# Second mixer: the product of probabilities and values from float32 to high and low parts in three passes

## The chip, the cores and the metric

One core of a Trainium2 chip runs the whole program once. The metric is the device time of that core in microseconds. Its five engines run programs of their own and meet at semaphores: TensorE (PE in the rows, with its weight loads as PEld), VectorE (DVE), ScalarE (ACT), GpSimd (POOL) and SyncE (SP), which issues the weight loads from memory.

## The reference, cut to what matters

Sequence 512, width 1024, float32 throughout. Two layers of feed-forward, mixer, feed-forward, and then a hybrid layer. The change lies in the mixer of the second layer, differential attention with 8 heads of width 128, where two softmaxes over 64-wide halves of queries and keys are subtracted and the difference multiplies the values:

```python
p1 = jax.nn.softmax(jnp.einsum('bhqd,bhkd->bhqk', q1b, k1) + bias, axis=-1)
p2 = jax.nn.softmax(jnp.einsum('bhqd,bhkd->bhqk', q2b, k2) + bias, axis=-1)
return jnp.einsum('bhqk,bhkv->bhqv', p1 - lam * p2, vh)
...
out = rms_norm(out, subln_g) * (1.0 - lam_init)
return out.reshape(B, S, DIFF_V).astype(h.dtype) @ w_out
```

## The kernel before

Activations lie transposed in SBUF, 128 features by 512 positions to a tile. A projection is made of units of 128 output columns. For a unit ScalarE copies 128x1024 raw weights into a float32r tile (`whi`, the high part), VectorE subtracts it from the raw weights (`wlo`, the low part), and TensorE does 24 matmuls of 512 columns in float32r: high by high, high by low, low by high. This scheme of parts is used for all projections and for the scores of the second mixer. The product of probabilities and values is not made so: its operands are plain float32.

The order of the second mixer is one list, `diff_steps()` (L231), which the programs of TensorE (L2322), ScalarE (L1062) and VectorE (L1704) each walk from front to back, doing their share of each step. Each engine is strictly in this order; a wait holds up all that stands behind it on its engine. A block n is 128 queries of head n // 4. The steps named below:

- `half`: 12 of the 24 matmuls of a projection unit (k, q or v of a head). After the second half VectorE makes the low part of a later weight unit (`w_lo`, L1334) and empties the bank (L1725 into `qb`, L1720 into `vt` for v). For k and q ScalarE squares the result.
- `ss`, `rs`, `qk`, `hi`, `lo`: TensorE sums the squares of q and k; ScalarE takes Ln and Exp of each sum (`rq`); VectorE scales (L1734); ScalarE copies six high parts (`hi`), VectorE subtracts four low parts (`lo`, L1746). `attend` of a new head needs these low parts.
- `attend` n: TensorE makes two score tiles of two matmuls each, VectorE adds the bias and takes the minimum (L1758), ScalarE exponentiates (L772).
- `comb` n: four VectorE instructions (L1787 to L1793) subtract the two softmaxes.
- `turn` n: TensorE turns the block in four transposes into one PSUM bank, and ScalarE empties the bank into its part of `DPT` (`sb_dif_pt`) and counts `d_pt`. The next `turn` needs the bank to be empty.
- `vT` h: TensorE turns the values (`dvt`), ScalarE empties the bank into `DV` and counts `d_vrow`.
- `pv` h: four float32 matmuls of `DV` and `DPT`; ScalarE squares the result. `oss` and `o` normalise it, `y` splits it for the output projection, whose rows are the steps `begin` and `more`.

From head 1 to head 5 the steps repeat, here with n = 4h:

```python
half("k", h + 1, 0)
steps += [("vT", h), ("attend", n), ("comb", n - 1), ("o", h - 2)]
half("k", h + 1, 1)
steps.append(("turn", n - 2))
half("q", h + 1, 0)
steps += [("attend", n + 1), ("comb", n), ("turn", n - 1)]
half("q", h + 1, 1)
steps += [("attend", n + 2), ("comb", n + 1), ("pv", h - 1), ("ss", h + 1)]
half("v", h + 1, 0)
steps += [("rs", h + 1), ("qk", h + 1), ("hi", h + 1), ("turn", n), ("attend", n + 3), ("comb", n + 2)]
half("v", h + 1, 1)
steps += [("lo", h + 1), ("oss", h - 1), ("turn", n + 1)]
```

GpSimd takes no part in this, save the loads of the bias. In the feed-forward parts it issues 75 accumulating DMAs within SBUF (L2600).

Of the kernel before, what the change touches and what calls it, by code (L numbers as in the profile page):

```python
# [51 lines left out]
NCOLS = _n  # L52
STAGE = 21792

# [347 lines left out]
d_hi_q d_hi_k d_lo_q d_lo_k d_v d_vT d_vrow  # L402
d_score d_max d_exp d_comb d_turn d_pt d_pv d_osq d_oss d_y d_yhi d_ylo
gs h_z h_hi h_conv0 h_conv h_gmm h_gates h_ri h_ix h_tanh h_a h_ln h_m h_sqrt h_one h_b h_scan
# [5 lines left out]
def build(nc, a):  # L410
    with ExitStack() as ctx:
# [74 lines left out]
        with ExitStack() as mem:  # L486
            def t_(name, shape, dt=F32):
                return sb("dif_" + name, shape, dt, mem)

            O = t_("y", [128, 8, S])  # L490
            bt = [t_(f"bias{i}", [128, 896]) for i in range(2)]
            qb = [t_(f"qb{i}", [128, S]) for i in range(2)]
            dsq = [t_(f"sq{i}", [128, S]) for i in range(2)]
            drq = [t_(f"rq{i}", [128, S]) for i in range(2)]
            dparts = [[t_(f"{n}{i}", [128, S], F32R) for n in ("q0", "q1", "k0", "k1", "kl0", "kl1")] for i in range(2)]
            dvt = t_("vt", [128, S])
            DV = [t_(f"v{i}", [128, 4, 128]) for i in range(2)]
            dpb = [[t_(f"p{i}{j}", [128, S]) for j in range(2)] for i in range(3)]
            DPT = t_("pt", [128, 4, S])
            dst = [t_(f"st{i}", [128, 8]) for i in range(3)]  # L500
# [255 lines left out]
        def act_program(e):  # L756
# [305 lines left out]
            def diff():  # L1062
                u = first["diff"]
                for s in DS:
# [41 lines left out]
                    elif s[0] == "vT":  # L1106
                        h = s[1]
                        w.wait_ge(sem["d_vT"], h + 1)
                        if h >= 2:
                            w.wait_ge(sem["d_pv"], h - 1)  # L1110
                        act(DV[h % 2][:, :, :], psum[DIF_MISC][:, :].rearrange("p (s c) -> p s c", c=128),
                            ACT.Copy).then_inc(sem["d_vrow"], 1)
                    elif s[0] == "attend":
# [6 lines left out]
                    elif s[0] == "turn":  # L1120
                        n = s[1]
                        w.wait_ge(sem["d_turn"], n + 1)
                        if n >= 4:
                            w.wait_ge(sem["d_pv"], n // 4)
                        act(DPT[:, :, n % 4 * 128:n % 4 * 128 + 128],
                            psum[DIF_TURN][:, :].rearrange("p (c q) -> p c q", q=128),
                            ACT.Copy).then_inc(sem["d_pt"], 1)
                    elif s[0] == "pv":
                        h = s[1]
                        w.wait_ge(sem["d_pv"], h + 1)  # L1130
                        if h:
                            w.wait_ge(sem["d_oss"], h)
                        act(sq[:, :], psum[DIF_PV][:, :], ACT.Square).then_inc(sem["d_osq"], 1)
                    elif s[0] == "oss":
                        h = s[1]
                        w.wait_ge(sem["d_oss"], h + 1)
                        if h:
                            w.wait_ge(sem["d_y"], h)
                        rsqrt_into(sqs[:, :], psum[DIF_MISC][:, :], 128, ("d_o", h))
# [173 lines left out]
        def dve_program(e):  # L1313
# [390 lines left out]
            def diff():  # L1704
                u = first["diff"]
                zero_halves(dparts)
                for s in DS:
                    if s[0] == "half":
                        _, tag, h, half = s
# [59 lines left out]
                    elif s[0] == "y":  # L1769
                        n = s[1]  # L1770
                        w.wait_ge(sem["d_yhi"], n + 1)
                        e.tensor_tensor(xl[:, n, :], O[:, n, :], xh[:, n, :].bitcast(F32),
                                        ALU.subtract).then_inc(sem["d_ylo"], 1)
                    elif s[0] == "begin" and s[1]:
                        w_lo(u)

            def zero_halves(parts):
# [200 lines left out]
        def pe_program(e):  # L1978
# [332 lines left out]
            def diff_misc_free(key):  # L2311
# [5 lines left out]
                elif key[0] == "vT":  # L2317
                    w.wait_ge(sem["d_vrow"], key[1] + 1)
                else:
                    w.wait_ge(sem["lnb"], ln_done(("q", key[1])))  # L2320

            def diff():  # L2322
                u = first["diff"]
                misc, in_free, got = None, [], {}
                for s in DS:
# [48 lines left out]
                    elif s[0] == "turn":  # L2374
                        n = s[1]
                        w.wait_ge(sem["d_comb"], 4 * n + 4)
                        if n:
                            w.wait_ge(sem["d_pt"], n)
                        turned(DIF_TURN, dpb[n % 3][0], 4, sem["d_turn"])
                    elif s[0] == "pv":  # L2380
                        h = s[1]
                        w.wait_ge(sem["d_vrow"], h + 1)
                        w.wait_ge(sem["d_pt"], 4 * h + 4)
                        if h:
                            w.wait_ge(sem["d_y"], h)
                        for c in range(4):
                            ins = mm(psum[DIF_PV][:, :], DV[h % 2][:, c, :], DPT[:, c, :], c == 0, c == 3)
                        ins.then_inc(sem["d_pv"], 1)
# [21 lines left out]
            def out_bank_free(m):  # L2410
# [7 lines left out]
                elif m == 5:  # L2418
                    w.wait_ge(sem["d_pt"], 32)
                elif m == 6:  # L2420
# [345 lines left out]
```

## Time and profile before

| | us |
|---|---|
| median of 3 runs (2163.63 to 2164.08) | 2163.75 |
| the profiled execution | 2163.63 |
| its span in the profile | 2161.8 |
| busy PE / PEld / DVE / ACT / POOL | 2144.5 / 1835.3 / 1680.9 / 1176.7 / 253.0 |
| share of the chain that ended last: PE, DVE, ACT | 91%, 4%, 2% |

Times in the rows are microseconds from the start of the span, those marked mean are ns. [...] A float32 matmul stands as two records. The second mixer lies between about 1310 and 1556 us, and its products stand at 1365.77, then every 27.94 us.

### The profile page before, as it was taken

The numbers are of one execution on the slowest core, as the hardware profiler recorded it, in microseconds if no ns is written. First come the engines' busy times: TensorE is split into PE (matmuls) and PEld (weight loads), VectorE is DVE, ScalarE is ACT, GpSimd is POOL, SyncE is SP. The second block draws the span as 40 slices with busy tenths as digits, with TensorE's granted clock in tenths as the row PEclk, the third lists the DMA queues.
The fourth block names the chain that finished last, engine by engine and source line by source line (L and its number), as shares of the span: only waits on it lengthen the run. The fifth ranks groups of instructions, "written<-read, shape, count | busy, mean of one in ns | idle before, by whom it ended". The sixth has DMA issues, their size and how long they took to land.

```text
span 2161.8 us, 33546 instructions
## 1 busy us (share of the span) xinstructions
PE 2144.5 (99%) x13412; PEld 1835.3 (85%) x13412; DVE 1680.9 (78%) x2546; ACT 1176.7 (54%) x1922; POOL 253.0 (12%) x187
## 2 busy tenths in 40 slices
PE   9999999999999999999999999999999999999999
PEld 6989897777779898989899997777789898977777
DVE  8789697988678796888787787777688886966873
ACT  6536264667556263546355356777555362638672
POOL 3000004000040000040010112000130000030000
PEclk9999999999999999999999999999999999999999
DMA  7454535131135555354554542222135545332211
GB/s 214 123 136 99 151 94 161 40 98 60 46 89 141 124 137 151 84 162 125 176 129 127 122 126 92 77 75 95 50 79 150 137 100 150 98 131 74 79 59 39
DMA packets 249451, 237.75 MB, mean 110 GB/s; under 512 B 4984, under 2 KB 245240, under 8 KB 249296
## 3 DMA queue, kind: packets, MB, share of 16 engines
q1 hardware_dynamic: 208336, 210.25, 30.3%
q0 software_dynamic: 40752, 25.11, 8.7%
q8 instruction: 107, 1.75, 0.3%
q14 instruction: 48, 0.39, 0.1%
q10 hardware_dynamic: 208, 0.24, 0.0%
HBM read 213.79 MB, written 6.32 MB: 102 GB/s over the span
## 4 chain that ended last, share of the span: by engine, by line
PE 91%; DVE 4%; ACT 2%; issue 1%; DMA 0%; SPq 0%; ACTq 0%; DVEq 0%
PE ps L1982 90%; PE ps L1986 1%; DVE sb_wlo L1334 1%; DMA sb_raw<-ffn_w_gu 0%; ACT sb_whi L771 0%; DVE sb_gla_ek L1689 0%; DVE sb_gla_eq L1692 0%; ACT sb_hyb_th L771 0%; ACT sb_lnb L771 0%; DVE sb_gla_cf L1681 0%; DVE sb_gla_xb L1684 0%; DVE sb_gla_d L1669 0%; SPq L737 0%; DVE sb_rb L1965 0%; ACT sb_xh L771 0%
## 5 line engine op out<-in xcount | busy, mean ns | idle before, releaser
L1982 PE MATMUL ps<-sb_xh,sb_whi 128*128 128x512 f32 (+1 forms) x1812 | 625.4, 345 | 3.6 <-issue 1.8
L1982 PE MATMUL ps<-sb_xl,sb_whi 128*128 128x512 f32 (+1 forms) x1812 | 608.8, 337 | 0.1
L1982 PE MATMUL ps<-sb_xh,sb_wlo 128*128 128x512 f32 (+1 forms) x1812 | 606.7, 337 | 0.0
L771 ACT ACTIVATE sb_whi<-sb_raw 128x1024 fp32r<-128x1024 f32 (+1 forms) x368 | 379.9, 1037 | 376.6 <-PE ps L1982 359.8
L1982 PEld LDWEIGHTS ps<-sb_xh,sb_whi 128*128 128x128 f32 x1812 | 344.0, 190 | 56.8 <-issue 20.4
L1982 PEld LDWEIGHTS ps<-sb_xl,sb_whi 128*128 128x128 f32 x1812 | 344.2, 190 | 39.3 <-DVE sb_xl L1354 3.3
L1982 PEld LDWEIGHTS ps<-sb_xh,sb_wlo 128*128 128x128 f32 x1812 | 343.9, 190 | 37.1
L1982 PE MATMUL ps<-sb_ffn_tl,sb_whi 128*128 128x256 f32 x1200 | 339.6, 283 | 0.0
L1982 PE MATMUL ps<-sb_ffn_th,sb_whi 128*128 128x256 f32 x1200 | 339.6, 283 | 0.0
L1982 PE MATMUL ps<-sb_ffn_th,sb_wlo 128*128 128x256 f32 x1200 | 339.6, 283 | 0.0
L1334 DVE TENSOR_TENSOR sb_wlo<-sb_raw,sb_whi 128x1024 fp32r<-128x1024 f32 (+1 forms) x218 | 275.6, 1271 | 49.1 <-ACT sb_whi L771 48.6
L1982 PE MATMUL ps<-sb_ffn_ah,sb_whi 128*128 128x512 f32 x704 | 275.4, 391 | 0.0
L1982 PE MATMUL ps<-sb_ffn_ah,sb_wlo 128*128 128x512 f32 x704 | 274.1, 389 | 0.0
L1982 PE MATMUL ps<-sb_ffn_al,sb_whi 128*128 128x512 f32 x704 | 274.1, 389 | 0.0
L1982 PEld LDWEIGHTS ps<-sb_ffn_tl,sb_whi 128*128 128x128 f32 x1200 | 230.4, 192 | 0.0
L1982 PEld LDWEIGHTS ps<-sb_ffn_th,sb_wlo 128*128 128x128 f32 x1200 | 230.4, 192 | 0.0
L1982 PEld LDWEIGHTS ps<-sb_ffn_th,sb_whi 128*128 128x128 f32 x1200 | 230.4, 192 | 0.0
L2600 POOL DMA_DIRECT2D sb_raw<-sb_raw x75 | 96.4, 1350 | 989.5 <-DMA sb_raw<-ffn_w_gu 736.2
L1327 DVE TENSOR_TENSOR sb_wlo<-sb_raw,sb_whi 128x1024 fp32r<-128x1024 f32 x150 | 182.7, 1218 | 2.4 <-ACT sb_whi L771 2.4
L771 ACT ACTIVATE sb_whi<-sb_ffn_sums 128x1024 fp32r<-128x1024 f32 (+1 forms) x150 | 125.7, 841 | 83.4 <-DVE sb_ffn_sums L1349 64.5
L1982 PEld LDWEIGHTS ps<-sb_ffn_ah,sb_wlo 128*128 128x128 f32 x704 | 132.1, 188 | 27.9
L1982 PEld LDWEIGHTS ps<-sb_ffn_ah,sb_whi 128*128 128x128 f32 x704 | 132.2, 188 | 26.9
(293 smaller groups left out, 2919.9 us busy)
## 6 DMA issues: line engine op xcount, KB each, us to landing
sb_raw<-ffn_w_gu SPq DMA_DIRECT2D x86, 1024.0 KB, 5.8
sb_raw<-ffn_w_down SPq DMA_DIRECT2D x32, 1024.0 KB, 5.1
sb_raw<-sb_raw POOLq DMA_DIRECT2D x75, 256.0 KB, 4.2
sb_raw<-w_ada SPq DMA_DIRECT2D x12, 1024.0 KB, 7.6
sb_raw<-ffn_w_down SPq DMA_DIRECT2D x16, 768.0 KB, 5.6
sb_raw<-gla_w_in SPq DMA_DIRECT2D x12, 1024.0 KB, 5.5
sb_raw<-diff_w_in SPq DMA_DIRECT2D x12, 1024.0 KB, 5.1
sb_raw<-w_in SPq DMA_DIRECT2D x10, 1024.0 KB, 5.1
```

What stands on the lines that cost most here:

```text
L771: return e.activation(out, in_, func, bias=bias, scale=scale)
L1327: e.tensor_tensor(lo, fast_source(u), hi.bitcast(F32), ALU.subtract).then_inc(sem["w_lo"], 1)
L1334: e.tensor_tensor(lo, raw[panel % NRAW][:, 0:nk, off:off + 128], hi.bitcast(F32), ALU.subtract).then_inc(sem["w_lo"], 1)
L1982: return e.matmul(out, lhsT, rhs, start=start, stop=stop, skip_group_check=skip)
L1986: ins = e.transpose(psum[bank][:, c * 128:(c + 1) * 128], src[:, c * 128:(c + 1) * 128], ident)
L2600: e.dma_start(raw[up % NRAW][:, 0:4, off:off + 128], raw[gate % NRAW][:, 0:4, off:off + 128], accum_op=ALU.add).then_inc(sem[f"s_pre{i % 2 ...
```

## The change

The values and the turned probabilities are kept as float32r high parts and float32r low parts, and the product becomes three float32r matmuls for each of the four blocks of keys. ScalarE empties each turned bank twice: into the high part (`DPT`, `DV`) and, exact, into a second tile (`dpw`, one buffer; for the values `dvt`, their own source). The next `turn` waits for both. VectorE subtracts the high part from the exact copy, 32 times for the probabilities (`low_probabilities`) and 8 times for the values (`low_values`), after the first `attend` or `comb` that follows the `turn` or `vT` in the list; the second copy into `dpw` waits for the subtraction of the block before. `pv` waits for the low parts. The count `d_pt` and `d_vrow` go by twos. The space for stages grows, and the memory kept for GpSimd's DMA descriptors is set to 2048 bytes a partition.

```diff
-STAGE = 21792
+STAGE = 25376
...
-            DV = [t_(f"v{i}", [128, 4, 128]) for i in range(2)]
+            DV, DVL = ([t_(f"{n}{i}", [128, 4, 128], F32R) for i in range(2)] for n in ("v", "vl"))
-            DPT = t_("pt", [128, 4, S])
+            DPT, DPTL = t_("pt", [128, 4, S], F32R), t_("ptl", [128, 4, S], F32R)
+            dpw = t_("pw", [128, 4, 128])
...
# ScalarE, vT and turn
+                        turned = psum[DIF_MISC][:, :].rearrange("p (s c) -> p s c", c=128)
+                        act(DV[h % 2][:, :, :], turned, ACT.Copy).then_inc(sem["d_vrow"], 1)
+                        act(dvt[:, :].rearrange("p (s c) -> p s c", c=128), turned, ACT.Copy).then_inc(sem["d_vrow"], 1)
...
+                        act(DPT[:, :, own], turned, ACT.Copy).then_inc(sem["d_pt"], 1)
+                        if n:
+                            w.wait_ge(sem["d_ptl"], n)
+                        act(dpw[:, :, :], turned, ACT.Copy).then_inc(sem["d_pt"], 1)
...
# VectorE
+                    if s[0] == "turn":
+                        if block is not None:
+                            low_probabilities(block)
+                        block = s[1]
+                    elif s[0] == "vT":
+                        head = s[1]
...
+                        if n == 6:
+                            low_probabilities(block)
+                            block = None
...
+                    if s[0] in ("attend", "comb"):
+                        if head is not None:
+                            low_values(head)
+                            head = None
+                        if block is not None:
+                            low_probabilities(block)
+                            block = None
+            def low_probabilities(n):
+                own = slice(n % 4 * 128, n % 4 * 128 + 128)
+                w.wait_ge(sem["d_pt"], 2 * n + 2)
+                e.tensor_tensor(DPTL[:, :, own], dpw[:, :, :], DPT[:, :, own].bitcast(F32),
+                                ALU.subtract).then_inc(sem["d_ptl"], 1)
+            def low_values(h):
+                w.wait_ge(sem["d_vrow"], 2 * h + 2)
+                e.tensor_tensor(DVL[h % 2][:, :, :], dvt[:, :].rearrange("p (s c) -> p s c", c=128), DV[h % 2][:, :, :].bitcast(F32),
+                                ALU.subtract).then_inc(sem["d_vlo"], 1)
...
# TensorE, turn and pv
-                            w.wait_ge(sem["d_pt"], n)
+                            w.wait_ge(sem["d_pt"], 2 * n)
...
-                        w.wait_ge(sem["d_vrow"], h + 1)
-                        w.wait_ge(sem["d_pt"], 4 * h + 4)
+                        w.wait_ge(sem["d_vlo"], h + 1)
+                        w.wait_ge(sem["d_ptl"], 4 * h + 4)
...
-                            ins = mm(psum[DIF_PV][:, :], DV[h % 2][:, c, :], DPT[:, c, :], c == 0, c == 3)
+                            mm(psum[DIF_PV][:, :], DV[h % 2][:, c, :], DPT[:, c, :], c == 0, False)
+                            mm(psum[DIF_PV][:, :], DV[h % 2][:, c, :], DPTL[:, c, :], False, False)
+                            ins = mm(psum[DIF_PV][:, :], DVL[h % 2][:, c, :], DPT[:, c, :], False, c == 3)
...
-    nc = bacc.Bacc("TRN2", target_bir_lowering=False, num_devices=1)
+    nc = bacc.Bacc("TRN2", target_bir_lowering=False, num_devices=1, dynamic_dma_scratch_size=2048)
```

## Rows read from the trace of the kernel before

**Rows 1.** Page, parts 1 and 2: busy time of the engines; granted TensorE clock in tenths.
```profile
PE 2144.5 (99%) x13412; PEld 1835.3 (85%) x13412; DVE 1680.9 (78%) x2546; ACT 1176.7 (54%) x1922; POOL 253.0 (12%) x187
PEclk9999999999999999999999999999999999999999
```

**Rows 2.** Windows: stretch, length, busy time of PE, PEld, DVE, ACT, POOL, clock, DMA.
```profile
1400.00:1440.00 40.00, 40.00 (x185) 29.87 (x184) 30.81 (x68) 32.61 (x62) 1.07 (x2) 1.00 0.32 102
```

**Rows 3.** Timeline of TensorE, one head: start, duration, engine, line, operation, tiles, count.
```profile
1392.78 0.39 PE L1982 MATMUL ps<-sb_dif_k,sb_dif_q 128*128 128x512 f32 x1
1393.01 0.39 PE L1982 MATMUL ps<-sb_dif_kl,sb_dif_q 128*128 128x512 f32 x1
...
1393.69 3.59 PE L1982 MATMUL ps<-sb_dif_pt,sb_dif_v 128*128 128x512 f32 x8
1397.21 1.09 PE L1982 MATMUL ps<-sb_dif_sq,sb_cst 64*64 64x512 f32 x8
...
1406.09 0.60 PE L1986 MATMUL ps<-sb_cst,sb_dif_p 128*128 128x128 f32 x4
...
1409.65 0.48 PE L1982 MATMUL ps<-sb_dif_k,sb_dif_q 128*128 128x512 f32 x1
...
1417.51 0.63 PE L1986 MATMUL ps<-sb_cst,sb_dif_p 128*128 128x128 f32 x4
...
1421.63 3.59 PE L1982 MATMUL ps<-sb_dif_pt,sb_dif_v 128*128 128x512 f32 x8
```

**Rows 4.** Timeline of ScalarE in the same head.
```profile
1401.39 2.58 ACT L771 ACTIVATE sb_dif_k<-sb_dif_qb 64x512 fp32r<-64x512 f32 x4
...
1405.31 0.60 ACT L771 ACTIVATE sb_dif_pt<-ps 128x512 f32<-128x512 f32 x1
1405.93 0.72 ACT L772 ACTIVATE sb_dif_p<-sb_dif_p,sb_dif_st 128x512 f32<-128x512 f32 x1
...
1415.60 1.28 ACT L771 ACTIVATE sb_dif_sq<-sb_dif_qb 64x512 f32<-64x512 f32 x2 [2.94 <-DVE sb_dif_qb L1725]
1416.79 0.57 ACT L771 ACTIVATE sb_dif_pt<-ps 128x512 f32<-128x512 f32 x1
```

**Rows 5.** Timeline of VectorE in the same head, with idle time before and its releaser.
```profile
1400.14 0.75 DVE L1734 SCALAR_TENSOR_TENSOR sb_dif_qb<-sb_dif_qb,sb_par,sb_dif_rq 128x512 f32<-128x512 f32 x1 [3.62 <-ACT sb_dif_rq L771]
...
1403.44 0.16 DVE L1787 RECIPROCAL sb_dif_st<-sb_dif_st 128x2 f32<-128x2 f32 x1
...
1404.90 1.22 DVE L1334 TENSOR_TENSOR sb_wlo<-sb_raw,sb_whi 128x1024 fp32r<-128x1024 f32 x1
1406.04 0.68 DVE L1720 TENSOR_TENSOR sb_dif_vt<-ps,sb_rb 128x512 f32<-128x512 f32 x1
...
1408.06 1.41 DVE L1746 TENSOR_TENSOR sb_dif_q<-sb_dif_qb,sb_dif_q 64x512 fp32r<-64x512 f32 x2
1410.40 0.69 DVE L1758 CUSTOM_DVE_ANT_0 sb_dif_p<-ps,sb_dif_bias 128x512 f32<-128x512 f32 x1 [0.93 <-PE ps L1982]
...
1414.88 0.68 DVE L1725 TENSOR_TENSOR sb_dif_qb<-ps,sb_rb 128x512 f32<-128x512 f32 x1
1417.25 0.69 DVE L1758 CUSTOM_DVE_ANT_0 sb_dif_p<-ps,sb_dif_bias 128x512 f32<-128x512 f32 x1 [1.69 <-PE ps L1982]
```

**Rows 6.** Timeline of VectorE near the end: a subtraction of the new one's form.
```profile
1519.78 1.90 DVE L1772 TENSOR_TENSOR sb_xl<-sb_dif_y,sb_xh 128x512 fp32r<-128x512 f32 x3 [1.01 <-ACT sb_xh L771]
```

**Rows 7.** Timeline of TensorE: the products of heads 0, 5, 6 and 7.
```profile
1365.77 3.59 PE L1982 MATMUL ps<-sb_dif_pt,sb_dif_v 128*128 128x512 f32 x8
...
1505.46 3.60 PE L1982 MATMUL ps<-sb_dif_pt,sb_dif_v 128*128 128x512 f32 x8
...
1531.49 3.59 PE L1982 MATMUL ps<-sb_dif_pt,sb_dif_v 128*128 128x512 f32 x8
...
1544.10 3.59 PE L1982 MATMUL ps<-sb_dif_pt,sb_dif_v 128*128 128x512 f32 x8
```

**Rows 8.** Page, part 5: GpSimd's accumulating DMAs, busy, mean ns, idle before.
```profile
L2600 POOL DMA_DIRECT2D sb_raw<-sb_raw x75 | 96.4, 1350 | 989.5 <-DMA sb_raw<-ffn_w_gu 736.2
```

More of the change, by code:

```diff
@@ L402 @@
 d_hi_q d_hi_k d_lo_q d_lo_k d_v d_vT d_vrow
-d_score d_max d_exp d_comb d_turn d_pt d_pv d_osq d_oss d_y d_yhi d_ylo
+d_score d_max d_exp d_comb d_turn d_pt d_ptl d_vlo d_pv d_osq d_oss d_y d_yhi d_ylo
 gs h_z h_hi h_conv0 h_conv h_gmm h_gates h_ri h_ix h_tanh h_a h_ln h_m h_sqrt h_one h_b h_scan
@@ L1110, in diff @@
                             w.wait_ge(sem["d_pv"], h - 1)
-                        act(DV[h % 2][:, :, :], psum[DIF_MISC][:, :].rearrange("p (s c) -> p s c", c=128),
-                            ACT.Copy).then_inc(sem["d_vrow"], 1)
+                        turned = psum[DIF_MISC][:, :].rearrange("p (s c) -> p s c", c=128)
+                        act(DV[h % 2][:, :, :], turned, ACT.Copy).then_inc(sem["d_vrow"], 1)
+                        act(dvt[:, :].rearrange("p (s c) -> p s c", c=128), turned, ACT.Copy).then_inc(sem["d_vrow"], 1)
                     elif s[0] == "attend":
@@ L1124, in diff @@
                             w.wait_ge(sem["d_pv"], n // 4)
-                        act(DPT[:, :, n % 4 * 128:n % 4 * 128 + 128],
-                            psum[DIF_TURN][:, :].rearrange("p (c q) -> p c q", q=128),
-                            ACT.Copy).then_inc(sem["d_pt"], 1)
+                        turned = psum[DIF_TURN][:, :].rearrange("p (c q) -> p c q", q=128)
+                        own = slice(n % 4 * 128, n % 4 * 128 + 128)
[3 more added lines that the diff above has]
+                        act(dpw[:, :, :], turned, ACT.Copy).then_inc(sem["d_pt"], 1)
                     elif s[0] == "pv":
@@ L1706, in diff @@
                 zero_halves(dparts)
+                block, head = None, None
                 for s in DS:
-                    if s[0] == "half":
+                    if s[0] == "turn":
[4 more added lines that the diff above has]
+                        head = s[1]
+                    elif s[0] == "half":
                         _, tag, h, half = s
@@ L1775, in diff @@
                         w_lo(u)
+                    if s[0] in ("attend", "comb"):
[6 more added lines that the diff above has]
+            def low_probabilities(n):
+                own = slice(n % 4 * 128, n % 4 * 128 + 128)
+                w.wait_ge(sem["d_pt"], 2 * n + 2)
[5 more added lines that the diff above has]
+                                ALU.subtract).then_inc(sem["d_vlo"], 1)
             def zero_halves(parts):
@@ L2317, in diff_misc_free @@
                 elif key[0] == "vT":
-                    w.wait_ge(sem["d_vrow"], key[1] + 1)
+                    w.wait_ge(sem["d_vrow"], 2 * key[1] + 2)
                 else:
@@ L2418, in out_bank_free @@
                 elif m == 5:
-                    w.wait_ge(sem["d_pt"], 32)
+                    w.wait_ge(sem["d_pt"], 64)
                 elif m == 6:
```

## Prediction

> **What bounds the kernel now.** I read the page first: TensorE is busy 99% of the span at the full granted clock [rows 1], so a microsecond taken from its queue is one gained, and any wait put into it is one lost. The windows view then says how near the others are in the stage of the change: of 40 us around one head TensorE is busy 40.00, VectorE 30.81, ScalarE 32.61 [rows 2]. Neither is a bound by its sum. But both walk the same hand-written list in order, so I went on to the three timelines of one head [rows 3 to 5]. There TensorE never waits, and the reader is to see how thin some margins are: `turn` at 1417.51 starts 0.15 us after the copy of 1416.79 (0.57 long) that empties its bank, and `attend` at 1409.65 starts 0.18 us after the last low part of q (1408.06 + 1.41) [rows 3 to 5]. Where VectorE idles it is for ScalarE (3.62) or for TensorE (0.93, 1.69) [rows 5].
>
> **What TensorE gains.** A product stands from 1393.69 to 1397.21, 3.52 us [rows 3]. Afterwards it is 12 float32r matmuls of the form of the scores, whose starts are 0.23 apart (1392.78, 1393.01; four in 0.91) [rows 3]: 2.75 us. Weight loads stay hidden, as there. Gain 0.77 us, eight times 6.2 us. If nothing else moved the time would be 2163.63 - 6.2 = 2157.4.
>
> **What ScalarE and VectorE get.** ScalarE: 40 more copies of 128x512 from PSUM, 0.57 to 0.60 us each [rows 4], 23 us; behind the first one the second ends 1.1 us after the first started (0.5 to 0.6 from start to start). VectorE: 40 subtractions of 128x512 into float32r, which is the form of the three in 1.90 us [rows 6]: (1.90 - 0.69) / 2 = 0.60 each in a row, 24 us, with 0.69 until the result is there. By busy time both fit into the idle time of rows 2. What decides is the places where they stand and wait.
>
> **Replay of one head.** I set the program orders side by side with these durations and let each instruction start when its engine and its inputs are free. Count from E, the end of the product (1397.21 now), with n = 4h. Now: VectorE scales k at E + 2.93 (1400.14) and ScalarE's six high parts run from E + 4.18 (1401.39) to E + 8.1, only then comes the copy of `turn` n (1405.31) [rows 4, 5]. VectorE has finished the minima of `attend` n + 3 at E + 6.2 (1403.44) and goes straight on with `comb` (1.46), `w_lo` (1.14), the values (0.60) and four low parts (2.83), done at 1409.47, E + 12.26 [rows 5].
>
> (1) The change puts `low_probabilities(n)` behind that `attend`, at E + 6.2, and it waits for ScalarE's second copy, which ends at E + 8.1 + 1.1 = E + 9.2. VectorE stands for 3.0 us with `comb` n + 2, `w_lo`, the values, and the four low parts queued behind it. They end at 9.25 + 0.60 + 1.46 + 1.14 + 0.60 + 2.83 = E + 15.9. TensorE loses 0.3 at `turn` n + 1 (now 1406.09, E + 8.88, then 9.2 for the bank), then does 12 matmuls of k (2.85 with the change from float32, to E + 12.5), waits 0.65 at `vT` for the values (E + 13.1), and starts `attend` of the new head at E + 16.0 instead of E + 12.44 (1409.65). Cost 3.6 us.
>
> (2) Count from this `attend`, A. Minima from A + 0.75 to 1.98; now `comb`, `o`, `w_lo` and the bank of k follow, which ends at A + 5.9 (1414.88 + 0.68). In between come `low_values` and `low_probabilities`, 1.2 us: A + 7.1. ScalarE's squares of k wait for it (2.94 idle now, releaser L1725) and take 1.19 (1415.60 to 1416.79), its first copy of `turn` n' - 2 (n' the new head's first block) starts at A + 8.3, the second ends at A + 9.4. `turn` n' - 1, now at 1417.51, A + 7.86, waits for that: 1.6 us more.
>
> (3) VectorE's minima of `attend` n' + 1 end at A + 8.8, the next subtraction waits for the same second copy and ends at 10.1; `comb`, `w_lo` bring 12.7, the bank of q 13.5 (TensorE ends its half at 12.65), the minima of `attend` n' + 2 14.7, and then comes the subtraction of block n' - 1, done at A + 15.4. TensorE is ready for the product at 9.5 + 0.35 + 2.8 + 0.9 = A + 13.55 and waits 1.9 us. It starts at A + 15.45; now 1421.63, A + 11.98. So (2) and (3) cost 3.5.
>
> Period: 2.75 + 16.0 + 15.45 = 34.2 against 27.94: +6.2 us, of which 7.0 are waits and 0.8 is returned. VectorE is reset in each head by its wait for `rq` (3.62 idle, rows 5), so this doesn't grow from head to head. Between the products of head 0 and head 5 (1365.77, 1505.46) [rows 7] lie five periods: +31.
>
> **Before the first product** the same two things happen: the second copy of block 0 stands ahead of Ln and Exp and makes the low parts of head 1 0.5 us later, for which TensorE waits; then `attend` 4, the second copies and both subtractions make the bank of k, its squares and the copies of block 2 late, so that `turn` 3 is 2.4 us late, and the subtraction of block 3 behind `attend` 6 adds 1.7. Product 0 starts 4.1 us late.
>
> **After product 5** (E now at 1508.99): the low parts of head 7 end at E + 12.7 as in (1), `attend` 28 is 3.1 us late. From there VectorE has a single chain without pause: y 0 to 2, minima 28, block 25, y 3, minima 29, the values, `comb` 27, block 26, `o` 5, y 4 and 5, two `w_lo`, `comb` 28, block 27, done at E + 29.3; product 6 is now at E + 22.5 (1531.49), so it is 6.8 late, with a wait of 3.7 us ahead of it. Product 7, now E + 35.1 (1544.10), comes at E + 42.4: the second copy of block 30 waits for the subtraction of block 29, and the last `turn` for that copy. From the start of product 5 to the end of product 7 it is 2.75 + 42.4 + 2.75 = 47.9 instead of 42.1 (1505.46 to 1544.10 + 3.52): +5.7. Behind it TensorE is full again, and the shift goes to the end.
>
> Sum: 4.1 + 31 + 5.7 = +41 us on the profiled execution's 2163.63 (span 2161.8 and 1.8 around it; the median is 0.12 above it): **2204.5 us**. What is left out: some 20 hand-offs a head at 0.05 to 0.1 each, of which I know the sum to perhaps 0.8 us a period. That makes 2197 to 2212.
>
> The space for stages costs nothing, since no tile of another stage is moved in time. ScalarE's copies into float32r (2.58 for four of 64x512, 0.65 each) stand near those into float32 (0.57 to 0.60 for 128x512) [rows 4]; with 0.65 the second copies would end 0.05 later, which is within the 0.8.
>
> **Rivals.** *Only the product waits* (0.08). If ScalarE came to its second copy of `turn` n by E + 6.2, the loss of (1) and (2) would be gone and only the subtraction behind `attend` n' + 2 would remain, 1.9 - 0.8 = 1.1 a head, with start and tail some 12 us: 2176. Against it speaks that the six high parts stand ahead of the copy and end at E + 8.1 [rows 4]. *Gain only* (0.03), the other side: the mechanism is VectorE's reserve, 9 us idle in 40. If each subtraction fell into one of the idle stretches (3.62, 0.93, 1.69), TensorE would keep its gain: 2157.4. It decides at E + 6.2 and at A + 12: both the second copy and the subtraction would have to be done before. The list puts them later. *The clock falls* (0.05): four waits a head of 0.3 to 2.5 us are new, where now the granted clock is full throughout [rows 1]. [...] *Descriptor memory* (0.02): with 2048 bytes GpSimd might have to wait for one DMA to land before the next. It has 989.5 us idle ahead of these 75 [rows 8]; if half of them reached TensorE with their own 1.35 us each, +50: 2255. *The replay holds, but stalls cancel to nothing* (0.02): 2163.
>
> [...]
>
> **Chances and range.** The forecast has 0.80. The range 2186 to 2220 holds it with its bounds; it is wider than the 2197 to 2212 of its own terms because one misplaced wait of 1.5 us a head counts six times (9 us), and because the first rival can hold in part. The 2176, the 2224 and all beyond are left out, 0.2 in sum. A measurement tells about 0.2% (4.3 us) from no change: slower 0.95, same 0.02, faster 0.03.
>
> **What would show it.** VectorE idle some 3 us ahead of the new subtraction, released by ScalarE's `pw`, once a head; TensorE idle ahead of `attend` of a new head (2.5), `turn` n' - 1 (1.6) and the product (1.9); products 34 us apart and 2.75 long; product 6 behind a wait of 3.7; all else of the span unchanged. It would be wrong if the products stood 28 us apart, if the subtraction took clearly more than 0.6, if the granted clock fell, or if the feed-forward parts grew.

## The result and the profile after

The changed kernel took 2213.32 us (median of 4 runs, 2209.97 to 2214.54) where the kernel before took 2163.69 (2163.6 to 2164.08): 1.0227 times as long, with a 95% interval of 1.021 to 1.0243. The profiled span went from 2161.8 to 2211.5 us, +49.7. Direction and mechanism were those of the forecast, the size was not quite: 41 us were forecast, and 2213.32 lies in the stated range but 1.3 above the 2197 to 2212 of its own terms.

The page of the changed kernel, parts 1 and 2, which answers to [rows 1]:

```profile
PE 2156.5 (98%) x13444; PEld 1848.0 (84%) x13444; DVE 1707.0 (77%) x2586; ACT 1197.4 (54%) x1962; POOL 253.6 (11%) x187
PEclk9999999999999999999999999999999999999999
```

VectorE got 26.1 us more and ScalarE 20.7, near the 24 and 23 of the forecast. TensorE should have become 6 us less busy and is 12.0 busier. The same matmuls without the waits (the first experiment below) make it 5.2 less busy, 2139.3. That is the first sign that it ran some slowly, though the row of the clock shows only nines at this resolution; the mean granted clock of the span is 0.995 where it was 1.000.

The windows view of the changed kernel, with stretches chosen around one wait of TensorE each; columns as in [rows 2]:

```profile
1389.00:1394.00 5.00, 4.96 (x15) 3.92 (x16) 4.00 (x11) 1.63 (x4) 0.00 (x0) 0.66 0.21 72
1394.00:1406.00 12.00, 9.67 (x46) 7.52 (x45) 10.00 (x23) 7.79 (x16) 0.00 (x0) 1.00 0.00 0
1406.00:1411.00 5.00, 5.00 (x19) 2.73 (x19) 0.64 (x1) 1.47 (x3) 0.00 (x0) 0.66 0.01 3
...
1440.00:1475.00 35.00, 28.29 (x130) 20.95 (x130) 24.51 (x53) 24.46 (x48) 0.54 (x1) 1.00 0.20 69
```

In the first and the third the mean granted clock is 0.66; there are seven such stretches, four in the periods of heads 1 to 5 and three behind product 5. The last row is the one period without any, from product 2 (1440.9) to product 3 (1475.3): it is 34.41 us long, the others 35.08 to 35.62. Its waits, the timeline of TensorE again, are the cleanest picture of the replay:

```profile
1440.91 0.47 PE L2017 MATMUL ps<-sb_dif_pt,sb_dif_v 128*128 128x512 f32 x1 [1.75 <-issue]
...
1459.74 0.50 PE L2017 MATMUL ps<-sb_dif_k,sb_dif_q 128*128 128x512 f32 x1 [2.03 <-DVE sb_dif_q L1758]
...
1469.29 0.63 PE L2021 MATMUL ps<-sb_cst,sb_dif_p 128*128 128x128 f32 x4 [1.52 <-ACT sb_dif_pw L772]
...
1475.32 0.47 PE L2017 MATMUL ps<-sb_dif_pt,sb_dif_v 128*128 128x512 f32 x1 [1.75 <-issue]
```

`attend` of the new head waits 2.03 us, `turn` n' - 1 then 1.52, the product 1.75, where 2.5, 1.6 and 1.9 were forecast. A wait in brackets begins where the record of the last matmul ends. As the records overlap (0.39 long, 0.23 apart), what a matmul takes is read from start to start, and the start behind a wait is late by some 0.2 us more than the wait says.

What a low clock means is seen between the products of heads 0 and 1, same view:

```profile
1370.21 0.47 PE L2017 MATMUL ps<-sb_dif_pt,sb_dif_v 128*128 128x512 f32 x1 [1.79 <-DVE sb_dif_ptl L1803]
...
1373.14 1.09 PE L2017 MATMUL ps<-sb_dif_sq,sb_cst 64*64 64x512 f32 x8
...
1389.04 0.50 PE L2017 MATMUL ps<-sb_dif_k,sb_dif_q 128*128 128x512 f32 x1 [2.02 <-DVE sb_dif_q L1758]
...
1390.40 0.63 PE L2017 MATMUL ps<-sb_xh,sb_whi 128*128 128x512 f32 x1
1390.82 0.63 PE L2017 MATMUL ps<-sb_xl,sb_whi 128*128 128x512 f32 x1
...
1393.49 0.40 PE L2017 MATMUL ps<-sb_xh,sb_wlo 128*128 128x512 f32 x1
1393.72 0.40 PE L2017 MATMUL ps<-sb_xh,sb_whi 128*128 128x512 f32 x1
...
1398.82 0.63 PE L2021 MATMUL ps<-sb_cst,sb_dif_p 128*128 128x128 f32 x4
...
1405.29 0.47 PE L2017 MATMUL ps<-sb_dif_pt,sb_dif_v 128*128 128x512 f32 x1 [2.19 <-issue]
```

The reader is to see three things. The product is twelve matmuls (1370.21 to 1373.14) behind a wait of 1.79 us for the low parts. `attend` of the new head waits 2.02 us for the low parts of q. And 0.7 us after that wait matmuls that started 0.23 us apart start 0.43 apart (1390.40, 1390.82), until 1393.1. The windows view of 1390 to 1393 gives a granted clock of 0.50 there, and the stretch from 1394 to 1406 shown before it 1.00.

What VectorE did meanwhile, its timeline:

```profile
1382.36 0.69 DVE L1803 TENSOR_TENSOR sb_dif_ptl<-sb_dif_pw,sb_dif_pt 128x512 fp32r<-128x512 f32 x1 [2.91 <-ACT sb_dif_pw L772]
...
1404.49 0.69 DVE L1803 TENSOR_TENSOR sb_dif_ptl<-sb_dif_pw,sb_dif_pt 128x512 fp32r<-128x512 f32 x1
```

It stood for 2.91 us ahead of `low_probabilities(n)`, with everything for the next head queued behind it. The second line is the last subtraction that the next product needs: it ends at 1405.18, and the product starts at 1405.29. The waits view of TensorE over the whole mixer (from 1300 to 1620 us) sums up what became of it: what is waited for, us in total, times, longest:

```profile
PE ps L2017 <- issue: 13.5, 6, 3.4
PE ps L2017 <- DVE sb_dif_q L1758: 12.3, 7, 2.0
PE ps L2021 <- ACT sb_dif_pw L772: 8.5, 10, 1.7
PE ps L2021 <- DVE sb_dif_vt L1732: 2.7, 5, 0.6
PE ps L2017 <- DVE sb_dif_ptl L1803: 1.8, 1, 1.8
```

The first row is that of the later products, put down to "issue" because several semaphores are waited for one after the other. Before 1310 us nothing moved: TensorE's busy time is 495.05 against 495.12 us in the first 500 us, and 498.89 in both kernels in the second 500.

### The profile page after: what moved, and what is told of

It reads as the page before. It is cut to its first block, busy times and chain, and to the rows that moved or that the text cites. A ratio compares the mean times of both kernels' runs of the same rounds, so it can differ in the third digit from the quotient of the medians.

```text
span 2211.5 us, 33699 instructions
## 1 busy us (share of the span) xinstructions
PE 2156.5 (98%) x13444; PEld 1848.0 (84%) x13444; DVE 1707.0 (77%) x2586; ACT 1197.4 (54%) x1962; POOL 253.6 (11%) x187
## 3 DMA queue, kind: packets, MB, share of 16 engines
q8 instruction: 107, 1.75, 0.3%
## 4 chain that ended last, share of the span: by engine, by line
PE 85%; DVE 7%; ACT 5%; issue 2%; DMA 0%; SPq 0%; DVEq 0%; ACTq 0%
PE ps L2017 84%; DVE sb_wlo L1339 1%; PE ps L2021 1%; ACT sb_dif_k L772 1%; ACT sb_whi L772 1%; ACT sb_lnb L772 1%; DVE sb_dif_q L1758 0%; DMA sb_raw<-ffn_w_gu 0%; DVE sb_dif_kl L1758 0%; DVE sb_gla_ek L1694 0%; DVE sb_gla_eq L1697 0%; ACT sb_dif_q L772 0%; ACT sb_dif_pw L772 0%; DVE sb_dif_ptl L1803 0%; DVE sb_dif_p L1770 0%
## 5 line engine op out<-in xcount | busy, mean ns | idle before, releaser
L2017 PEld LDWEIGHTS ps<-sb_ffn_al,sb_whi 128*128 128x128 f32 x704 | 132.2, 188 | 26.8
```

Of the source, the lines that this page charges most:

```text
L2017: return e.matmul(out, lhsT, rhs, start=start, stop=stop, skip_group_check=skip)
```

## The experiments

All are the changed kernel with an edit, but for the last, which is the kernel before with one. The edits are cut to their main lines. The medians are us; a ratio is to the kernel before on the same chip.

**The product alone.**

```diff
-                        act(DPT[:, :, own], turned, ACT.Copy).then_inc(sem["d_pt"], 1)
-                        if n:
-                            w.wait_ge(sem["d_ptl"], n)
-                        act(dpw[:, :, :], turned, ACT.Copy).then_inc(sem["d_pt"], 1)
+                        act(DPT[:, :, own], turned, ACT.Copy).then_inc(sem["d_pt"], 2)
...
+                for t in (DVL[0], DVL[1], DPTL):
+                    e.memset(t[:, :, :].bitcast(F32), 0.0).then_inc(sem["d_ptl"], 1)
...
             def low_probabilities(n):
...
-                w.wait_ge(sem["d_pt"], 2 * n + 2)
-                e.tensor_tensor(DPTL[:, :, own], dpw[:, :, :], DPT[:, :, own].bitcast(F32),
-                                ALU.subtract).then_inc(sem["d_ptl"], 1)
+                pass
```

> Leaves out: the second copies of ScalarE and all 40 subtractions; the low parts are zero, so the product is that of the high parts alone, in the same twelve matmuls. Theory (what is lost is lost at waits for ScalarE and VectorE, TensorE itself gains 0.77 us a product): 2157 to 2158 us, products 2.75 long and 27.2 us apart, no fall of the granted clock, feed-forward parts as before in spite of the smaller descriptor memory. Rival (the three passes or the descriptor memory cost time themselves): at or above 2163.7.

Measured: 2159.83, ratio 0.9983 (0.9973 to 0.9992), 1.8 above the expected stretch. The timeline of TensorE of this run:

```profile
1367.32 0.39 PE L2011 MATMUL ps<-sb_dif_pt,sb_dif_v 128*128 128x512 f32 x1
...
1370.13 1.09 PE L2011 MATMUL ps<-sb_dif_sq,sb_cst 64*64 64x512 f32 x8
...
1394.51 0.39 PE L2011 MATMUL ps<-sb_dif_pt,sb_dif_v 128*128 128x512 f32 x1
```

The product stands 2.81 us, and the five periods are 27.19 to 27.24, on average 0.72 under the 27.94 of before (forecast 0.77). Over eight products that is near 6 us; 1.5 of them went into the three memsets at the start of the mixer, which make the first product late (1367.3 where 1365.8 was before). The experiment adds these itself, and they are why the expected stretch was missed. So the matmuls of the change pay what was said, and all the rest of the 49.6 us is in what feeds them.

**The second copies, without the subtractions.**

```diff
-                        if n:
-                            w.wait_ge(sem["d_ptl"], n)
...
             def low_probabilities(n):
...
-                w.wait_ge(sem["d_pt"], 2 * n + 2)
-                e.tensor_tensor(DPTL[:, :, own], dpw[:, :, :], DPT[:, :, own].bitcast(F32),
-                                ALU.subtract).then_inc(sem["d_ptl"], 1)
+                pass
```

> Leaves out: the 40 subtractions of VectorE (low parts zero). ScalarE makes both copies, turn waits for both. Theory: the copies alone cost little, 0.3 at turn n+1 and 0.4 at turn n'-1 a head, 0.5 at the start, 1 in the tail: 2162 to 2165 us. Rival (ScalarE's 23 us of copies are the cost, since its chain Ln, Exp, high parts is what TensorE waits for): above 2180.

Measured: 2167.88, 1.0019 (1.001 to 1.0029), 8.0 above the product alone and 3 above what I had expected. Its waits view of TensorE:

```profile
PE ps L2017 <- ACT sb_dif_pw L772: 5.4, 13, 1.2
```

Thirteen short waits for the second copy. The period is 28.2, 1.0 over that of the product alone. Two `turn`s a head come just behind the copy of the one before and now have a copy more to wait for: each stands idle for 0.3 us and starts 0.5 late. The sum of 0.7 a head that was expected counted 0.3 and 0.4.

**The subtractions, without the second copies.**

```diff
-                        act(DPT[:, :, own], turned, ACT.Copy).then_inc(sem["d_pt"], 1)
-                        if n:
-                            w.wait_ge(sem["d_ptl"], n)
-                        act(dpw[:, :, :], turned, ACT.Copy).then_inc(sem["d_pt"], 1)
+                        act(DPT[:, :, own], turned, ACT.Copy).then_inc(sem["d_pt"], 2)
...
-                e.tensor_tensor(DPTL[:, :, own], dpw[:, :, :], DPT[:, :, own].bitcast(F32),
+                e.tensor_tensor(DPTL[:, :, own], DPT[:, :, own].bitcast(F32), DPT[:, :, own].bitcast(F32),
```

> Leaves out: ScalarE's second copies; VectorE subtracts the high part from itself (zero), at the same places, waiting for the first copy. Theory: VectorE still stands at the subtraction of block 4h, for a copy that lies behind the six high parts, and the queue behind it is the same; only 0.5 us less at each of the waits for a second copy: period 33.1 instead of 34.2 undisturbed, 2195 to 2205 us, the upper end if the clock falls in as many spells. Rival (the second copies and their single buffer are the cost): near 2160.

Measured: 2206.5, 1.0198 (1.0183 to 1.0213), 46.7 above the product alone; a little above the expected stretch. VectorE's and TensorE's timelines of this run:

```profile
1381.91 0.69 DVE L1799 TENSOR_TENSOR sb_dif_ptl<-sb_dif_pt 128x512 fp32r<-128x512 f32 x1 [2.42 <-ACT sb_dif_pt L772]
```
```profile
1388.60 0.50 PE L2013 MATMUL ps<-sb_dif_k,sb_dif_q 128*128 128x512 f32 x1 [2.02 <-DVE sb_dif_q L1754]
...
1404.84 0.47 PE L2013 MATMUL ps<-sb_dif_pt,sb_dif_v 128*128 128x512 f32 x1 [2.49 <-issue]
```

VectorE now stands 2.42 us for the first copy instead of 2.91 for the second, and TensorE waits in the same places. The three parts nearly add up: -4.1, +8.0 and +46.7 make +50.6, and the whole change costs 49.6. The product alone holds 1.5 us for memsets that this run doesn't have, so that the subtractions cost 48 rather than 46.7; seven falls of the clock are in it, as in the change. The subtraction itself is 0.6 us; that its place is the cost, and not the work, is what the next runs ask.

**The subtraction of block n behind the low parts.** Only `low_probabilities(n)` of the heads' first blocks is moved, behind `lo`:

```diff
-                        if block is not None:
+                        if block is not None and not (block % 4 == 0 and 4 <= block < 28):
...
+                    if s[0] == "lo" and s[1] > 1:
+                        low_probabilities(block)
+                        block = None
```

> The changed kernel, with the subtraction of blocks 4, 8 .. 24 put behind the low parts of q and k instead of ahead of comb; nothing left out. Theory: cost (1), the 3 us in which VectorE stands with the low parts behind it, is gone, (2) and (3) stay: 3.1 less a head in six heads, 18.5, and some of the clock's fall with it: 2188 to 2195 us, attend of a new head 12.9 after the product's end. Rival (the time is in VectorE's total work, not in the place): unchanged, 2213.

Measured: 2201.56, 1.0175 (1.016 to 1.019): 12 us better than the change, where 18 to 25 were expected. `attend` of the new head came at E + 12.9 as expected, so step (1) of the forecast is shown:

```profile
1373.16 1.09 PE L2020 MATMUL ps<-sb_dif_sq,sb_cst 64*64 64x512 f32 x8
...
1386.07 0.48 PE L2020 MATMUL ps<-sb_dif_k,sb_dif_q 128*128 128x512 f32 x1
```

But ScalarE and then TensorE waited elsewhere:

```profile
1386.16 0.60 ACT L772 ACTIVATE sb_dif_pw<-ps 128x512 f32<-128x512 f32 x1 [0.54 <-DVE sb_dif_ptl L1806]
...
1393.88 1.28 ACT L772 ACTIVATE sb_dif_sq<-sb_dif_qb 64x512 f32<-64x512 f32 x2 [3.81 <-DVE sb_dif_qb L1737]
```
```profile
PE ps L2024 <- ACT sb_dif_pw L772: 16.6, 13, 2.2
```

With one buffer `dpw`, a later subtraction holds up the next second copy, and the waits for `pw` grow from 8.5 to 16.6 us. In a period with a full clock the next `turn` waits 2.2 us instead of 1.5, and the period is 32.05 against 34.41: 2.4 us won and not 3.1. I had replayed the place that I moved and not the ones behind it. The rest of the shortfall is the clock: it still fell in three of the five periods, and these are 33.66 to 33.69 long, 1.6 more than the other two. No later wait took that up.

**The same waits, filled.** This one asks of what the excess over 41 us is made. TensorE does matmuls on parts of q and k, whose results nobody reads, into a bank that is free, ahead of two waits of a head (`attend` and the product) and of that of product 6:

```diff
+                        if n % 4 == 0 and n >= 4:
+                            old = dparts[(h + 1) % 2]
+                            w.wait_ge(sem["d_max"], 2 * n - 2)
+                            for _ in range(8):
+                                mm(psum[DIF_RING[2 * n % 3]][:, :], old[0][:, 0:128], old[2][:, :], True, True)
...
+                            for _ in range(14 if h == 6 else 6):
+                                mm(psum[DIF_PV][:, :], now[0][:, 0:128], now[2][:, :], True, True)
```

> The changed kernel, with matmuls of no use (8 into the score bank ahead of the wait for a new head's low parts, 6 into the product's bank ahead of the wait for the last subtraction, 14 there for head 6) that take the place of idle time; all results as before. Theory: the 8.6 us by which the changed kernel exceeds the replay are TensorE at the lower clock level after waits; with the waits filled the granted clock stays at full and the time is the replay's: 2203 to 2207 us, spells of lower clock gone or nearly. Rival (the replay missed waits, the clock matters nothing): 2213 or more, the filler hidden.

Measured: 2206.69 (2206.44 to 2206.91), 1.0197 (1.018 to 1.0214). TensorE does more and the kernel is 6.6 us faster. Its windows view and timeline of TensorE in the same head:

```profile
1389.00:1394.00 5.00, 5.00 (x24) 4.14 (x25) 4.21 (x11) 1.52 (x4) 0.00 (x0) 1.00 0.19 66
```
```profile
1386.68 2.09 PE L2017 MATMUL ps<-sb_dif_k,sb_dif_q 128*128 128x512 f32 x8
1388.95 0.50 PE L2017 MATMUL ps<-sb_dif_k,sb_dif_q 128*128 128x512 f32 x1 [0.18 <-DVE sb_dif_q L1758]
...
1398.51 0.63 PE L2021 MATMUL ps<-sb_cst,sb_dif_p 128*128 128x128 f32 x4 [1.50 <-ACT sb_dif_pw L772]
...
1404.51 0.50 PE L2017 MATMUL ps<-sb_dif_pt,sb_dif_v 128*128 128x512 f32 x1 [0.34 <-DVE sb_dif_ptl L1803]
```

The clock stays at 1.00, and `attend` starts where it did, 0.1 us apart (1388.95 against 1389.04), but the product of head 1 at 1404.51 instead of 1405.29. The five periods are 34.37 to 34.42, and the one period of the changed kernel in which the clock stayed full, without any filler, was 34.41. So the filler itself moves nothing, and what the other periods had above that, 0.7 to 1.2 us, is the clock. This is the replay as the forecast had it.

**`turn` n' - 2 before the first half of k ends.**

```diff
+            steps.append(("turn", n - 2))
             half("k", h + 1, 1)
-            steps.append(("turn", n - 2))
```

> The changed kernel with turn n-2 ahead of the second half of k in heads 2 to 6, so that ScalarE's two copies stand ahead of the squares of k. Theory: the wait of 1.6 us ahead of turn n'-1 goes, but the product's wait grows from 1.9 to 2.5, since VectorE's queue is what ends last: 1.0 us less a head, 2205 to 2210. Rival (each wait adds up by itself): 1.6 a head, 8 us less, about 2204 or below.

Measured: 2214.64, 1.0233 (1.0218 to 1.0248): a miss, no better than the change. TensorE's timeline and waits of this run:

```profile
1403.46 0.47 PE L2017 MATMUL ps<-sb_dif_pt,sb_dif_v 128*128 128x512 f32 x1 [2.51 <-issue]
...
1404.96 0.63 PE L2017 MATMUL ps<-sb_dif_pt,sb_dif_v 128*128 128x512 f32 x1
1405.39 0.63 PE L2017 MATMUL ps<-sb_dif_ptl,sb_dif_v 128*128 128x512 f32 x1
```
```profile
PE ps L2017 <- issue: 16.0, 6, 3.4
PE ps L2021 <- ACT sb_dif_pw L772: 5.3, 7, 1.7
```

The wait for `pw` is gone in most heads and the first period, 33.43, is 1.0 under the 34.4 of the filled run, as expected. But TensorE only arrives earlier at the product and waits longer there (2.51 against 2.19, in sum 16.0 against 13.5), the matmuls behind it soon start 0.43 us apart (1404.96, 1405.39; granted clock 0.50 from 1405 to 1408), and the other periods are 34.7 to 36.7. In each of these the clock fell once or twice, six times in all against four in the change, and nearly every fall shows in full: 34.7 and 35.0 with one, 36.7 with two. The gain went to the clock.

**The product later**, behind `ss`, half 0 of v, `rs` and `qk` of the next head, so that its subtraction has time:

```diff
-        steps += [("attend", n + 2), ("comb", n + 1), ("pv", h - 1), ("ss", h + 1)]
+        steps += [("attend", n + 2), ("comb", n + 1)]
         half("v", h + 1, 0)
+        steps.append(("ss", h + 1))
...
-        steps += [("rs", h + 1), ("qk", h + 1), ("hi", h + 1), ("turn", n), ("attend", n + 3), ("comb", n + 2)]
+        steps += [("rs", h + 1), ("qk", h + 1), ("pv", h - 1), ("hi", h + 1), ("turn", n), ("attend", n + 3), ("comb", n + 2)]
...
```

> The changed kernel with the order second scores, first half of v, sums of squares, product (heads 1 to 6), so that the product is not asked for before its last subtraction. Theory: the wait of 1.9 us ahead of the product goes; 1.6 us a period remain, since ScalarE's chain to the low parts starts 0.3 later than it would by TensorE alone: about 10 us less, and fewer spells of lower clock: 2198 to 2205.

Measured: 2201.13, 1.0171 (1.0156 to 1.0186), as expected. Its waits view of TensorE:

```profile
PE ps L2018 <- DVE sb_dif_q L1759: 12.3, 7, 2.0
PE ps L2022 <- ACT sb_dif_pw L773: 12.2, 12, 1.7
PE ps L2018 <- issue: 3.4, 1, 3.4
```

The six waits ahead of products (13.5 us) are down to one, that of product 6; the periods are 32.8 to 33.5. Step (3) was real. The move is worth 12 us: 8 of them are the five periods at a full clock (32.8 against 34.4), and the clock fell five times instead of seven.

**All three moved.** The subtractions get steps of their own in the list (`lowp`, `lowv`), each where its inputs are long there: that of block n behind `lo` of the next head, the others behind the half unit after their `turn`; `turn` n' - 2 is early and the product late.

```diff
+            steps += [("lowp", n - 3), ("lowv", h)]
...
+        steps += [("attend", n + 1), ("lowp", n - 2), ("comb", n), ("turn", n - 1)]
...
+        steps += [("attend", n + 2), ("lowp", n - 1), ("comb", n + 1)]
...
+        steps += [("lo", h + 1), ("lowp", n), ("oss", h - 1), ("turn", n + 1)]
```

> All work of the change kept, in new places: turn n-2 ahead of the second half of k, each subtraction where VectorE is idle and its copy is there (block 4h behind the low parts, block 4h+1 and the values behind the bank of k), the product behind the first half of v, two weight low parts later in the tail. Theory (the cost is the places, not the 47 us of new work): TensorE is the bound again, period 27.3 to 28.0, tail 1 to 3 over before, granted clock full: 2159 to 2166 us. Rival (VectorE and ScalarE are too full to take the work, 30.8 and 32.6 busy of 40 before): above 2175.

Measured: 2171.23, 1.0034 (1.0022 to 1.0046). The same work as the change's, with 42 of its 49.6 us gone, and still 7 over the kernel before, 5 more than expected. Windows and waits of this run:

```profile
1400.00:1440.00 40.00, 38.60 (x181) 29.82 (x182) 33.18 (x68) 35.23 (x66) 1.08 (x2) 1.00 0.30 102
```
```profile
PE ps L2010 <- ACT sb_dif_pw L774: 7.1, 8, 1.6
```

The clock is at 1.00 throughout this run's mixer and the period is 28.05; 27.2 would be free of waits. What is left of it is one wait of 0.70 us a head for the second copy of `turn` n, and some hand-offs. That the period is within 0.1 us of the 27.94 of before shows the places as the cost: the work of both engines is the same as in the change. It also shows where the 7 us are, namely not there. `attend` 8, behind product 0, is 2.4 late (1384.13 against 1381.72), the four periods to `attend` 24 add 0.5, and the tail behind it 4.3.

**That `turn` later.** The kernel with all three moved; to give ScalarE time, `turn` n + 1 goes behind the first half of k, and `turn` 2 back to its old place. The first line with a minus is that of the changed kernel, the second that of all three moved:

```diff
-            steps += [("vT", h), ("attend", n), ("comb", n - 1), ("o", h - 2)]
+            steps += [("turn", n - 3), ("vT", h), ("attend", n), ("comb", n - 1), ("o", h - 2)]
...
-        steps += [("lo", h + 1), ("lowp", n), ("oss", h - 1), ("turn", n + 1)]
+        steps += [("lo", h + 1), ("lowp", n), ("oss", h - 1)]
```

> The kernel of the new places (e8), with turn n+1 behind the first half of k, so that it isn't asked for before ScalarE's second copy of block n, and turn 2 back in its old place. Theory: the 0.7 us a head that TensorE waits in e8 go, and 1.4 at the start: period 27.3 to 27.5 instead of 28.06, 5 us less than e8: 2165 to 2168 us. Rival (ScalarE is the bound of the period): period stays at 28.0.

Measured: 2170.98, 1.0031 (1.002 to 1.0043), a miss. The wait has moved to the next `turn`, which now comes too soon behind it (1380.87 and 1383.66); timeline of TensorE:

```profile
1383.66 0.63 PE L2010 MATMUL ps<-sb_cst,sb_dif_p 128*128 128x128 f32 x4 [0.83 <-ACT sb_dif_pw L774]
...
1545.88 0.63 PE L2010 MATMUL ps<-sb_cst,sb_dif_p 128*128 128x128 f32 x4 [1.90 <-DVE sb_dif_p L1815]
```

Product 0 comes 1.6 us earlier than with all three moved, as expected at the start; the five periods are 28.22 instead of 28.06 and take 0.8 of it back, and what follows product 5 is 1.1 longer. There the clock fell once behind the wait of 1.90. In the run with all three moved the same wait stood at the same step, and the clock stayed full. The wait in that run, and the windows from 1547 to 1550 of this run and of that one:

```profile
1546.66 0.63 PE L2010 MATMUL ps<-sb_cst,sb_dif_p 128*128 128x128 f32 x4 [1.90 <-DVE sb_dif_p L1815]
```
```profile
1547.00:1550.00 3.00, 2.71 (x8) 1.90 (x8) 1.60 (x3) 2.89 (x6) 0.00 (x0) 0.50 0.00 0
1547.00:1550.00 3.00, 2.43 (x13) 1.51 (x12) 1.79 (x4) 2.59 (x5) 0.00 (x0) 1.00 0.02 8
```

**The tail too.** The run before it with another order behind head 5: `turn` 25 behind `attend` 28, product 6 behind `turn` 28, the last values and the two `w_lo` later. The lines with a minus are those of the changed kernel:

```diff
-              ("begin", 1, 4), ("turn", 27), ("comb", 28), ("attend", 30), ("more", 0, 6), ("pv", 6), ("comb", 29),
+              ("begin", 1, 4), ("turn", 27), ("comb", 28), ("lowp", 27), ("attend", 30), ("more", 0, 6), ("comb", 29),
-              ("turn", 28), ("attend", 31), ("more", 1, 6), ("comb", 30), ("comb", 31), ("turn", 29),
+              ("turn", 28), ("pv", 6), ("attend", 31), ("comb", 30), ("lowp", 28), ("more", 1, 6), ("turn", 29), ("comb", 31),
...
```

> e9 with the tail in another order: turn 25 behind attend 28, product 6 behind turn 28, the last values and the two weight low parts later. Theory: waits of 1.6, 1.1 and part of 1.9 us go, 2 to 4 us less than e9: 2162 to 2165 us. Rival (VectorE is the bound of the tail, its order doesn't matter): as e9.

Measured: 2170.7, 1.0032 (1.0019 to 1.0044), a miss as well. The timeline of TensorE in the tail:

```profile
1544.39 0.63 PE L2010 MATMUL ps<-sb_cst,sb_dif_p 128*128 128x128 f32 x4 [1.93 <-DVE sb_dif_p L1815]
1546.35 0.47 PE L2006 MATMUL ps<-sb_xh,sb_whi 128*128 128x512 f32 x1 [0.47 <-DVE sb_wlo L1341]
```

The wait ahead of product 6 is gone and others stand in its place. Between products 5 and 7 there are six for VectorE, 5.1 us in sum, and two for ScalarE's second copy, 2.1 us. That fits the rival, that VectorE bounds the tail whatever the order, but does not show it: one order more was tried.

**The memory alone**, on the kernel before:

```diff
-STAGE = 21792
+STAGE = 25376
...
-    nc = bacc.Bacc("TRN2", target_bir_lowering=False, num_devices=1)
+    nc = bacc.Bacc("TRN2", target_bir_lowering=False, num_devices=1, dynamic_dma_scratch_size=2048)
```

> The kernel before, with only the larger space for stages and the descriptor memory of 2048 bytes. Theory: no change, 2163 to 2165 us. Rival (GpSimd waits for room for descriptors): over 2165, with longer or later landings of its 75 DMAs.

Measured: 2163.71 against 2163.78, 0.9999 (0.999 to 1.0008). The rival of the descriptor memory is out.

## Why the prediction was right, and where it fell short

- **The bound.** Right. TensorE had no wait to give away, and every wait put into its queue came out at the end.
- **The gain of the product.** Forecast 0.77 us each; 0.72 a period with the product alone, where it stands 2.81. Where the product follows a wait its first matmul takes 0.31 to the next start and not 0.23 (1370.21 to 1370.52), and the whole stands 2.93 (1370.21 to 1373.14) and not 2.75.
- **Step (1).** Right. VectorE stood 2.91 us (forecast 3.0), `vT` waited 0.53 (0.65), `attend` of the new head 2.02 (2.5) and started 15.90 after the product's end (16.0). That it is VectorE's place in the list and not its load was shown by moving this one subtraction: `attend` at E + 12.9.
- **Step (2).** Right where the clock is full: from product 2 to product 3 `turn` n' - 1 waits 1.52 us (forecast 1.6) and starts 9.55 after `attend` (9.5). In the head shown before it the matmuls ahead of it were slow, and it starts at 9.78 (1398.82) with no wait at all: the slow matmuls used up the time in which it would have waited.
- **Step (3).** Right in kind. The product starts 15.58 after `attend` where the clock is full (1475.32 behind 1459.74; forecast 15.45), 15.56 with the waits filled, and 16.25 where it fell.
- **The sum.** With the waits filled the three terms are: the first product 4.3 late (forecast 4.1), five periods 172.0 instead of 139.7, +32.3 (forecast 31), and the rest +6.3 (forecast 5.7); together 42.9, against 41. The 2 us are in part the product behind a wait (0.18 each), the rest I put down to hand-offs, which the forecast had put within 0.8 us a period.
- **The tail.** Product 6 stood behind a wait of 3.41 us, where 3.7 was forecast.
- **The step that was missing.** In the changed kernel the terms are 4.4, 35.6 and 9.6, and the last two are too large by 3.3 each against the run with the waits filled, 6.6 us in all. That is the granted clock, and a fall of it was one of the signs by which the forecast said it would be wrong. The forecast had it as a rival of 0.05, whose 2224 lies some 19 us above the 2204.5, in place of a term of its own. Both halves of that were off. The clock fell seven times in the mixer, so it should have stood in the sum; and no run shows the 19 us, an estimate of mine. The runs showed a third of it in its place. One fall holds 3.4 us (from 1389.7 to 1393.1 matmuls 0.43 apart, granted clock 0.50), 1.7 lost; seven make 12. And 5 of these came out of waits that TensorE would have had anyway, as at `turn` n' - 1. In the five periods the four falls stood behind waits of 2.02, 2.19, 2.02 and 2.03 us. What a fall cost in time depended on what followed: 6.6 us for the seven here, and the full 1.6 each in the run with the subtraction behind `lo` (periods of 33.66 to 33.69 against 32.05). That the measured time is still in the range is in part luck, since with 19 us for the clock in place of 6.6 it would not be.
- **The rivals.** "Only the product waits" needed the second copy by E + 6.2; VectorE's 2.91 us ahead of it exclude that. "Gain only" is what the product alone gave (2159.8), with no second copy and no subtraction; with both in better places it was not reached (2171). Descriptor memory cost nothing (2163.71 against 2163.78). That the stalls cancel to nothing is excluded by the 49.6.
- **What should be unchanged** was: TensorE's busy time ahead of the mixer is the same within 0.1 us.

What stays open is the last 7 us over the kernel before, and the 4 us that the product alone gains. In the three orders tried a wait for the second copy of 0.7 to 0.8 us a head remained and only moved; it eats what the product gains in a period. ScalarE is busy 35.2 of 40 us there, and each `turn` needs two copies in a row. Whether an order without that wait exists, or whether a second bank for `turn` would do it, was not tried. The 7 us over the kernel before are the start and the tail, and the two further orders took 1.6 us off the start and left the whole time where it was.

## What to carry to other kernels

An engine with 9 idle us in 40 can still not take one instruction of 0.6 us at a place where its input isn't there yet: what counts is what stands queued behind it. When the list is written by hand, give added work a step of its own, and put it where its input is long finished; here that took back 42 of 49.6 us with the same work. Replay every place that a moved step touches, since the wait taken from one place came back at the next in four of the runs, and put the clock's fall into the sum as soon as a saturated TensorE gets waits of some 2 us a head: in the changed kernel seven falls stood behind waits of 1.90 to 3.41 us and cost 6.6 us.

## What the runs showed of the hardware that I had not expected

The clock fell behind single waits of about 2 us. In the changed kernel TensorE was busy but for waits of 0.29, 0.53 and 2.02 us since the product of head 0, and 0.7 us after the last of these its matmuls started 0.43 us apart instead of 0.23, at a granted clock of 0.50; behind the 2.19 us wait of the next product the same, 1.5 us later. Each fall of this kernel held 3.4 us at 0.50; in the run with the subtraction behind `lo` one that began within the wait of 3.39 us ahead of product 6 held 6.9 us (1565.5 to 1572.4). No rule by the length of one wait follows: from 1440.9 to 1475.3 `attend` waits 2.03 us and the clock stays full. With the subtraction behind `lo`, five `turn`s waited 2.19 to 2.22 us, and the clock fell behind three of them. In the tail a wait of 1.90 us by itself left it full with all three moved, and in the next run the same wait at the same step was followed by a fall 1.1 us later. What decides between two such waits is not shown here. The orders with waits of 0.7 to 0.8 us in a period of 28 had a full clock in the stretch of the heads, as had the run in which filler matmuls left waits of 0.18, 1.50 and 0.34 us besides the shorter ones of 0.3 and 0.5.

In the changed kernel, where waits for other engines followed, the falls cost less than their slow matmuls: 12 us of slowness became 6.6 us of time. With the subtraction behind `lo` none followed that took it up, and each cost the whole 1.6 (33.66 against 32.05). And it made an improvement vanish: `turn` n' - 2 moved early took 1.0 us from the first period and nothing from the kernel, since TensorE then waited longer ahead of the product (2.51 us against 2.19) and the clock fell behind it.

The cost of matmuls whose results nobody uses was negative: 106 more of them in the kernel (13550 against 13444), and 6.6 us less (2206.69 against 2213.32).
